# A hybrid layer's RWKV pairs: values centred while they are turned, a gate in rounded products, and eight steps joined to others

## What is computed

```python
g = jax.nn.sigmoid(gd) @ f32(g2)                 # gate, rank 160
...
y = wkv7_scan(rh, heads(decay), kh, vh, -kk, kk * ah)
mean = jnp.mean(y, axis=-1, keepdims=True)       # over the 64 of a head
var = jnp.mean(jnp.square(y - mean), axis=-1, keepdims=True)
y = (y - mean) * lax.rsqrt(var + LNX_EPS)
y = y.reshape(B, L, D_RWKV) * f32(lnx_w) + f32(lnx_b)
bonus = jnp.sum(rh * kh * f32(r_k), axis=-1, keepdims=True) * vh
y = (y + bonus.reshape(B, L, D_RWKV)) * g
```

## Time and profile before

| | |
|---|---|
| median of 3 runs | 2562.8 us (2559.62 to 2563.7) |
| the profiled execution | 2557.35 us |
| its span | 2555.8 us |
| PE busy | 2460.7 us, 96% |
| DVE, ACT, POOL busy | 1131.4, 792.2, 170.0 us |
| mean granted clock of PE | 0.986 of full |

### The profile page before, as it was taken

How to read it: one execution, slowest core, us unless ns; L and a number is a source line. 1 busy time by engine, 2 the same in 40 slices (tenths; PEclk the granted TensorE clock), 3 DMA queues, 4 the chain that set the end, 5 groups by cost and what they waited for, 6 DMA issues and landing times.

```text
span 2555.8 us, 44106 instructions
## 1 busy us (share of the span) xinstructions
PE 2460.7 (96%) x16486; PEld 2067.5 (81%) x16486; DVE 1131.4 (44%) x1721; ACT 792.2 (31%) x1306; POOL 170.0 (7%) x190
## 2 busy tenths in 40 slices
PE   6999999999999779999999999999999999999997
PEld 6988888889888658888888888888888888888886
DVE  6356466475574654453333333233333333332343
ACT  6434334244243322243222132232232222221333
POOL 3001011010010012200000000000000000000033
PEclk8999999999999889999999999999999999999999
DMA  7242342332423443333323323333233233233332
GB/s 202 72 91 72 85 93 75 86 85 70 92 73 92 103 143 105 92 89 108 91 82 107 90 87 103 90 96 101 82 102 95 82 107 91 86 103 90 95 95 91
DMA packets 502951, 242.08 MB, mean 95 GB/s; under 512 B 98400, under 2 KB 495840, under 8 KB 502304
## 3 DMA queue, kind: packets, MB, share of 16 engines
q1 hardware_dynamic: 498352, 226.10, 32.6%
q0 software_dynamic: 4480, 14.17, 1.6%
HBM read 223.29 MB, written 16.92 MB: 94 GB/s over the span
## 4 chain that ended last, share of the span: by engine, by line
PE 81%; DVE 10%; DMA 3%; ACT 2%; issue 2%; SPq 1%; DVEq 0%; ACTq 0%
PE PD L1293 63%; PE PD L1296 12%; DMA uni<-inverse 1%; DVE uni L1104 1%; DVE uni L976 1%; DMA inverse<-UU 1%; PE PW L1408 1%; DMA yin<-mixed 1%; DVE w_lo L902 1%; DVE uni L1049 0%; DVE uni L1043 0%; DVE act_lo L907 0%; PE PW L1415 0%; PE PW L1454 0%; PE PW L1353 0%
## 5 line engine op out<-in xcount | busy, mean ns | idle before, releaser
L902 DVE TENSOR_TENSOR w_lo<-w_raw,w_hi 128x512 fp32r<-128x512 f32 x780 | 556.1, 749 | 305.4 <-ACT w_hi L650 294.0
L650 ACT CAST w_hi<-w_raw 128x512 fp32r<-128x512 f32 x780 | 456.5, 619 | 752.4 <-PE PD L1293 484.6
L1293 PE MATMUL PD<-act_hi,w_hi 128*128 128x512 f32 x1408 | 557.6, 396 | 5.2 <-DVE act_lo L951 5.2
L1293 PE MATMUL PD<-act_lo,w_hi 128*128 128x512 f32 x1408 | 558.4, 397 | 0.0
L1293 PE MATMUL PD<-act_hi,w_lo 128*128 128x512 f32 x1408 | 555.4, 394 | 0.0
L1293 PE MATMUL PD<-u_hi,w_hi 128*128 128x512 f32 x1024 | 409.7, 400 | 0.0
L1293 PE MATMUL PD<-u_hi,w_lo 128*128 128x512 f32 x1024 | 403.3, 394 | 0.0
L1293 PE MATMUL PD<-u_lo,w_hi 128*128 128x512 f32 x1024 | 401.5, 392 | 0.0
L1296 PE MATMUL PD<-act_hi,w_hi 128*128 128x264 f32 x1376 | 312.7, 309 | 11.4 <-DVE act_lo L907 10.2
L1293 PEld LDWEIGHTS PD<-act_hi,w_hi 128*128 128x128 f32 x1408 | 265.8, 189 | 70.3 <-DVE act_lo L951 6.4
L1293 PEld LDWEIGHTS PD<-act_lo,w_hi 128*128 128x128 f32 x1408 | 265.5, 189 | 61.7 <-issue 0.7
(11 more groups left out here) (251 smaller groups left out, 1464.9 us busy)
## 6 DMA issues: line engine op xcount, KB each, us to landing
w_raw<-in_w_up SPq DMA_DIRECT2D x256, 256.0 KB, 3.1
w_raw<-in_w_down SPq DMA_DIRECT2D x256, 256.0 KB, 2.9
w_raw<-in_w_in SPq DMA_DIRECT2D x200, 256.0 KB, 3.0
w_raw<-in_w_out SPq DMA_DIRECT2D x64, 256.0 KB, 2.7
x_rows<-in_x SPq DMA_DIRECT2D x4, 1024.0 KB, 8.0
residual<-res POOLq DMA_DIRECT2D x2, 2048.0 KB, 11.3
out<-rows SPq DMA_DIRECT2D x8, 512.0 KB, 4.9
uni<-inverse SPq DMA_DIRECT2D x16, 240.0 KB, 4.2
```

The lines of the kernel that those rows point to most:

```text
L650: nc.scalar.copy(w_hi[:, q % RING], w_raw[:, q % RAW]).then_inc(hi_split, 1)
L902: V.tensor_tensor(w_lo[:, q % RING], w_raw[:, q % RAW], w_hi[:, q % RING].bitcast(F32), ALU.subtract).then_inc(lo_split, 1)
L1293: ins = M(pd_seq(n), w, v[:, k, first:first + SEQ], start=begin, stop=end)
```

## The change

- PE turns the values by a product with `centre` (identity less the head mean) where it transposed them. The step `mean`, ACT's copy of y and DVE's `yc` go; ACT squares y out of PSUM, and `y1` reads y from PSUM.
- The gate's two fp32 products become four fp32r products (high by high, high by low, low by high, and the last 32 rows with their three parts stacked as one). They move into the step `var`, behind the variance's product and ahead of its signal. ACT and DVE split the gate's weights for each pair (`ghi`, `glo`). The 32 tail columns are loaded three times (12 loads for 4 at the start, three for one in each pair).
- `bsum`, `btr` and `ktr` become `tr`; `atr` and `mv` become `amv`; `tt16` goes into `t16`, `e` into `gh`, `mean` goes and `gate` goes into `var`.
- `lnb` is added to the bonus by ACT (`bonb`), so DVE's `y3` goes. A root on one number (`for_sqrt`) is put ahead of `sq`.
- DVE shifts the values in `ss`, behind `ssm`. PE's `ss` now also waits for DVE's `kk`.
- `PACE` places steps anew: `ss` 2, `low` 6, `vtr` 11, `gram0` 24, `tr` 26, `gram1` 29, `amv` 31, `x16` 54, `gh` 67, `y0` 72, `z8` 88, `y` 91, `var` 96.

```diff
-PACE = dict(ss=2, low=4, vtr=5, ahead0=5, gram0=7, bsum=1, btr=1, atr=1, ktr=1, gram1=1, mv=2, base1=0, base2=1,
-            ahead1=1, ahead2=4, ahead3=4, ahead4=4, ahead5=5, x16=2, t16=2, tt16=1, x32=2, tt32=2, pq=3, gh=3, e=1, y0=5,
-            z2=3, z3=2, z4=1, z5=2, z6=1, z7=2, z8=2, y=2, mean=3, var=4, gate=4)
+PACE = dict(ss=2, low=4, vtr=5, ahead0=6, gram0=7, tr=2, gram1=3, amv=2, base1=0, base2=0, ahead1=2, ahead2=4,
+            ahead3=4, ahead4=4, ahead5=4, x16=5, t16=2, x32=3, tt32=2, pq=3, gh=3, y0=5, z2=4, z3=2, z4=2, z5=2, z6=2,
+            z7=2, z8=2, y=3, var=5)
...
-ACT_STEPS = ["sq", "nrm", "for_sig", "sigw", "siga", "for_exp", "vtok", "epv", "em", "ep", "gs", "btok", "atok", "ktok", "mv", "x16", "x32",
-             "warm", "pq", "y", "sqc", "std"]
+ACT_STEPS = ["for_sqrt", "sq", "nrm", "for_sig", "sigw", "siga", "for_exp", "vtok", "epv", "em", "ep", "gs", "ghi", "btok",
+             "ktok", "bonb", "atok", "mv", "x16", "x32", "warm", "pq", "sqc", "std"]
 DVE_STEPS = (["kk", "ssm", "inv", "ld", "scan", "mid", "mu", "epv", "gs", "kkn", "tfac", "kp",
-              "at", "b", "bt", "rt", "kt", "rb", "gram0", "bon", "gram1", "diag"]
+              "at", "b", "bt", "rt", "kt", "rb", "gram0", "bon", "glo", "gram1", "diag"]
              + [f"{s}{m}" for m in (2, 4, 8) for s in ("pr", "ar", "pl", "al")] + ["ut"]
-             + ["t16", "tt16", "tt32", "gt", "hb", "e", *Z_STEPS, "yc", "inv2", "y1", "y2", "y3", "y4"])
+             + ["t16", "tt16", "tt32", "gt", "hb", "e", *Z_STEPS, "inv2", "y1", "y2", "y4"])
...
-SPLIT_FIRST = ("low", "base1", "base2", "x16", "y", "mean", "var")
-
-
-
-OUT_PACE = dict(pq=1, gh=1, z2=1, z3=1, z4=1, z5=1, z6=1, z7=1, z8=1, mean=2, var=2, gate=2)
+SPLIT_FIRST = ("low", "base1", "base2", "x16", "y", "var")
+
+
+
+OUT_PACE = dict(pq=1, gh=1, z2=1, z3=1, z4=1, z5=1, z6=1, z7=1, z8=1, y=2, var=4)
...
     low_wa = m_sb("low_wa", [P, T])
-    low_g = m_sb("low_g", [P, T])
-    low_g2 = m_sb("low_g2", [GATE_TAIL, T])
+    low_r = lambda name, n: sb(name, [P, n], F32R, on=mix)
+    low_hi, low_lo, low_tail = low_r("low_hi", SEQ), low_r("low_lo", SEQ), low_r("low_tail", SEQ)
     wa_w = m_sb("wa_w", [P, P])
     g_w = m_sb("g_w", [P, P])
-    g_w2 = m_sb("g_w2", [GATE_TAIL, P])
+    g_w2 = m_sb("g_w2", [P, P])
+    g_hi, g_lo, g_tail = low_r("g_hi", P), low_r("g_lo", P), low_r("g_tail", P)
...
-    ybuf, ycen = uni[:, 4 * W:4 * W + SEQ], uni[:, 4 * W + SEQ:4 * W + 2 * SEQ]
+    ycen = uni[:, 4 * W + SEQ:4 * W + 2 * SEQ]
+    low_g, low_g2 = em, epv[0:TAIL]
...
         sp.wait_ge(raw_zeroed, 1)
         for first, width in ((LOWR + 2 * P, GATE_TAIL), (LOWR, P), (LOWR + P, P)):
             for a in range(4):
-                load(win_q[a, :, :, first:first + width], q, width=width)
+                for copy in range(0, TAIL if width == GATE_TAIL else 1, GATE_TAIL):
+                    load(win_q[a, :, :, first:first + width], q, first=copy, width=width)
...
+        const(nc.gpsimd.tensor_tensor(centre[:], ident[:], head_mean[:], ALU.subtract))
...
-            pool.dma_start(g_w2[:], gate_g2[P:P + GATE_TAIL, bass.ts(j, P)]).then_inc(g_loaded, 16)
+            for first in range(0, TAIL, GATE_TAIL):
+                pool.dma_start(g_w2[first:first + GATE_TAIL, :], gate_g2[P:P + GATE_TAIL, bass.ts(j, P)]).then_inc(g_loaded, 16)
...
-            act.wait_ge(raw_loaded[q % RAW], at(16 * (q // RAW + 1), 16 * per // RAW, it))
+            act.wait_ge(raw_loaded[q % RAW], at(16 * (q // RAW + 3), 16 * per // RAW, it))
...
                 if name == "ss":
+                    done("for_sqrt", nc.scalar.activation(warm[:], eps_t[:, 0:1], ACT.Sqrt))
                     done("sq", nc.scalar.activation(fsq, zk[:], ACT.Square, scale=feat("k_k")))
...
-                if name == "btr":
-                    pe("btr")
-                    done("btok", nc.scalar.copy(b_tok[:].rearrange("p c n -> p (c n)"), turned(0)))
-                if name == "atr":
-                    pe("atr")
+                if name == "ahead0":
+                    act.wait_ge(g_loaded, at(64, 64, j))
+                    nc.scalar.copy(g_hi[:], g_w[:])
+                    done("ghi", nc.scalar.copy(g_tail[:], g_w2[:]))
+                if name == "tr":
+                    pe("tr")
+                    done("btok", nc.scalar.copy(b_tok[:].rearrange("p c n -> p (c n)"), in_row(0)))
+                    done("ktok", nc.scalar.copy(k_tok[:].rearrange("p c n -> p (c n)"), in_row(1)))
+                    dve("bon")
+                    done("bonb", nc.scalar.activation(bonus[:], bonus[:], ACT.Identity, bias=feat("lnb")))
+                if name == "amv":
+                    pe("amv")
                     done("atok", nc.scalar.copy(AMV[:, :, :, 0:HS], PW[:, 2:4, 0:W].rearrange("p h (c n) -> p h c n", c=SLOTS)))
-                if name == "ktr":
-                    pe("ktr")
-                    done("ktok", nc.scalar.copy(k_tok[:].rearrange("p c n -> p (c n)"), turned(0)))
-                if name == "mv":
-                    pe("mv")
                     done("mv", nc.scalar.copy(AMV[:, :, :, HS:P], PW[:, 0:2, 0:W].rearrange("p h (c n) -> p h c n", c=SLOTS)))
...
-                    done("y", nc.scalar.copy(token_order(ybuf), by_bank(2)))
-                if name == "mean":
-                    dve("yc")
-                    done("sqc", nc.scalar.activation(ysq, ycen, ACT.Square))
+                    done("sqc", nc.scalar.activation(token_order(ysq), by_bank(2), ACT.Square))
                 if name == "var":
                     pe("var")
-                    done("std", nc.scalar.activation(ysq, PW[:, 2, :], ACT.Sqrt, bias=eps_t[:, 1:2]))
+                    done("std", nc.scalar.activation(ysq, PW[:, 0, :], ACT.Sqrt, bias=eps_t[:, 1:2]))
...
+            if n == 3:
+                dve.wait_ge(low_top, 1)
+                r = slice(2 * GATE_TAIL, TAIL)
+                V.tensor_tensor(low_tail[r, :], low_g2[r, META:T], low_tail[r, :].bitcast(F32), ALU.subtract).then_inc(low_done, 1)
+            if n == 4:
+                dve.wait_ge(low_top, 2)
+                V.tensor_tensor(low_lo[:], low_g[:, META:T], low_hi[:].bitcast(F32), ALU.subtract).then_inc(low_done, 1)
...
+                    dve.wait_ge(z_done, at(5, 3, j))
                     done("kk", V.tensor_scalar(kk, zk[:], feat("k_k"), None, ALU.mult))
                     pe("ss")
                     done("ssm", V.tensor_scalar(halves(fsq), pw(2), 1e-24, None, ALU.max))
+                    shift(5, zv[:, PAD:TP], par[:, bass.ds(j + (PAR["mu"] + 16), 1)], 3, j)
                     act("nrm")
                     done("inv", V.reciprocal(fsq, fsq))
...
+                if name == "tr":
+                    pe("tr")
+                    done("bon", V.tensor_tensor(bonus[:], PW[:, 3, :], zv[:, PAD + META:TP], ALU.mult))
+                    act("ghi")
+                    r = slice(GATE_TAIL, 2 * GATE_TAIL)
+                    V.tensor_tensor(g_tail[r, :], g_w2[r, :], g_tail[r, :].bitcast(F32), ALU.subtract)
+                    done("glo", V.tensor_tensor(g_lo[:], g_w[:], g_hi[:].bitcast(F32), ALU.subtract))
...
-                if name == "mean":
-                    pe("mean")
-                    done("yc", V.tensor_tensor(ycen, ybuf, PW[:, 0, :], ALU.subtract))
                 if name == "var":
                     act("std")
                     done("inv2", V.reciprocal(ysq, ysq))
-                    done("y1", V.tensor_tensor(ycen, ycen, ysq, ALU.mult))
-                    done("y2", V.tensor_scalar(ycen, ycen, feat("lnw"), feat("lnb"), ALU.mult, ALU.add))
-                    done("y3", V.tensor_tensor(ycen, ycen, bonus[:], ALU.add))
-                if name == "gate":
-                    pe("gate")
-                    done("y4", V.tensor_tensor(bt[:, PAD + META:TP], ycen, PW[:, 0, :], ALU.mult))
+                    done("y1", V.tensor_tensor(token_order(ycen), by_bank(2), token_order(ysq), ALU.mult))
+                    act("bonb")
+                    done("y2", V.scalar_tensor_tensor(ycen, ycen, feat("lnw"), bonus[:], ALU.mult, ALU.add))
+                    done("y4", V.tensor_tensor(bt[:, PAD + META:TP], ycen, PW[:, 1, :], ALU.mult))
...
+                    dve("kk")
...
-                    ins = turn(0, lambda cols: zv[:, cols])
+                    pe.wait_ge(z_done, at(6, 3, j))
+                    for k in range(SLOTS):
+                        ins = M(PW[:, k // 4, k % 4 * P:(k % 4 + 1) * P], zv[:, k * P:(k + 1) * P], centre[:], start=True, stop=True)
...
+                if name == "tr":
                     dve("gram0")
-                    ins = M(PW[:, 2, :], same_head[:], ld[:, 0:SEQ], start=True, stop=True)
-                if name == "btr":
-                    ins = turn(0, lambda cols: bt[:, cols])
-                if name == "atr":
-                    dve("bon")
+                    M(PW[:, 3, :], same_head[:], ld[:, 0:SEQ], start=True, stop=True)
+                    for i in range(2 * SLOTS):
```

(58 more changed lines are left out.)

42 lines of the change are left out of this document (18 added, 24 removed).

## The result

The changed kernel took 2575.8 us (median of 5, 2574.12 to 2576.37) against 2562.8 us (median of 5, 2559.62 to 2566.66) for the kernel before: ratio 1.0051, 95% interval 1.0036 to 1.0066. It is 13 us slower. I had forecast 2561 with a range up to 2571; the case "slower" had 0.24. The span of the profiled run of after is 2574.8 us, that of before 2555.8 us. That is 19 us, more than the medians show, because the profiled run of before was 5.4 us under its median and that of after lies at its median.

The account below looks back on a forecast made before the run. PE's work (96% busy) and `var`'s place against the next pair bound it. Six loop intervals +3.3, first pair -5, last pair +5, -4, -2, start +0.5: -2 on 2557.35, 2555; median 5.4 above, 2561; range 2546 to 2571.

Parts of the forecast that it names:

- the case "slower": Rival: late chain delays `gram0`, the gram exchange and `x16`; decides from 1.0 us per pair, +9, 2570; chance 0.24.
- The wait at ss: T is when PE has made its 96 k-steps; PE waits 6.0 us for `kk`, `ss` starting at T + 9.3.
- From ss to gram0: PE's work and DVE's chain each take 19.5 us between `ss` and `gram0`; lower clock adds 1.9 in each pair.
- clock does not cost it: Rival: lower stretches fall inside the wait or `gram0` has reserve; seven pairs save 1.9 each, -13, 2548; chance 0.20.
- They meet: At `gram0`, PE's work and DVE's chain both arrive 19.5 us behind `ss`, so PE's wait there goes.
- From gram0 to the next T: Clean pair: `ss` to the next T (PE's 96 k-steps made) takes 91.1 us, of which 19.5 lie ahead of `gram0`.
- Less 1.4 (of 1.5 at `x16`, to which PE now has 23 k-steps): At `x16`: 1.4 of the 1.5 us wait goes, with 23 k-steps from `amv` where it had 21 from `mv`.
- the joined steps: Five joins of PE steps save 0.9 us a pair together, with 0 and 1.6 as ends.
- a sign of being wrong: Wrong if waits at `ss` were under 4 us, the clock stayed up, or `x16` still waited 1.5 us.
- The first pair: No `var` ahead, so no wait for `kk`: -6.1 us, taken as -5 since its `gram0` wait may have been smaller.
- The last pair: `x16` near T + 58: +5; `y` ahead of the last two loads: -4; work behind `y`: -2.
- joined steps save more: Rival: joins reach the upper bound of 1.6, with cheaper entries of `x16` and `y0`: -8, 2553; chance 0.18.

Follow-up runs that it names:

- e1: The changed kernel with `var` (variance's product and gate) three k-steps ahead of the pair's end; 2555.9 us, ratio 0.9982 to the kernel before.
- e9: The changed kernel with `var` three k-steps earlier, `ss` waiting for `y1` instead of `kk`, and the gate behind the k-steps following `var`; 2528.5 us, ratio 0.9864.
- e8: The changed kernel with `x16` and everything from it to `gh` one k-step later, taken out ahead of `y0`; 2574.6 us, ratio 1.0041.
- e11: The changed kernel with one join undone: `tt16`'s 32 small products in a step of their own one k-step behind `t16`; 2581.2 us, ratio 1.0068.
- e5: The kernel before the change with one wait more: its `ss` waits for `kk`; 2572.8 us, ratio 1.0044.
- e6: The changed kernel with `ss` waiting for `y1`, last reader of y's banks, by its own count instead of for `kk`; 2551.8 us, ratio 0.9959.
- e7: The changed kernel with the gate's four products in a step of their own behind `var`, so `std` waits for the variance's product alone; 2566.2 us, ratio 1.0017.

## Why the prediction was wrong, by its own steps

By the medians the kernel takes 15 us more than forecast (2575.8 against 2561). By the two profiled executions it is 21: the sum came to -2, and the span grew by 19, with some 5 us of that because the profiled execution of before was a quick one. The steps below go by the traces.

**The wait at ss: right.** Predicted: `ss` at T + 9.3, a wait of 6.0 us in seven pairs. Measured: T + 9.67, and 42.0 us in seven pairs with the 5.2 behind the jump.

**From ss to gram0: right, clock included.** 19.5 and 1.9 for the clock made 21.4; measured 21.76. Both parts are borne out: without a lower stretch it is 19.8 (e1's pair from 728.59, e9's 19.90), with it 1.9 more. The rival "clock does not cost it" is out. The Trainium skill (TensorE: Matmul & The Clock Gate, Part 1) has a kernel in which every wait for data is followed by a throttled stretch with a cost of its own. The trace agrees: behind each of the seven waits the clock fell, for 1.9 us, and in e9 this is gone with the wait. "They meet" at `gram0` was right as well: its waits are 0.2 at the most.

**From gram0 to the next T: the step that failed.** Predicted 71.6 (91.1 less 19.5), measured 73.36 (the pair 104.79 less 9.67 and 21.76). "Less 1.4 (of 1.5 at `x16`, to which PE now has 23 k-steps)" counted a gain twice. Beside it I took off 0.8 behind `gram0` and the joined steps (three of the five lie ahead of `x16`, some 0.5). Those bring PE to `x16` earlier, and `x16` stands where the inverse lands: 29.5 us behind `gram0` in the clean pair of before (366.94 below, less the 337.41 of the earlier trace rows), 29.60 in after with two k-steps more ahead of it, 29.63 in e8 with three more. The two k-steps filled 1.5 us of a wait of 1.5 to which 1.3 was added. So PE still waits there, 0.9 to 1.9 us (1.3 in the mean of seven) where 0.1 was forecast, close to the 1.5 that the prediction named as a sign of being wrong. PE's timeline of before in that pair:

```profile
366.94 0.69 PE L1389 MATMUL PW<-uni 64*64 64x64 f32 x32 [1.36 <-DMA uni<-inverse]
```

`t16`'s 0.3 to 0.4 for ACT's copy is a new wait, and takes back what the join of `tt16` gives (e11: 0.33).

A smaller term was put at nothing without a reason. The forecast compared a pair that is clean but for the stretch behind `ss` with the mean of before, 101.75, which lies 0.6 over its clean pairs because two have a lower stretch. After has one again: from T = 312.70 `gram0` to T is 74.84, with a lower clock behind the wait of 1.89 at `x16`; in the other five it is 72.9 to 73.4. So of the 1.76 about 0.3 is that stretch, and 1.5 the double count with `t16`'s wait.

Per pair of the loop: 0.36 + 0.36 + 1.76 = 2.5 us over the forecast of 102.3, 15 us in six.

**The first pair**: predicted -5, measured -2.9 (T at 208.76 against 211.33, less the 0.3 of the start below), the same double count once.

**The last pair**: predicted -1, measured about +4. T to the end of `y4` was 108.9 us (821.82 to 930.69) and is 112.6 (837.50 to 950.13). PE's timeline has `x16` there:

```profile
897.08 1.12 PE L1409 MATMUL PW<-uni 64*64 64x64 f32 x32 [4.03 <-DMA uni<-inverse]
```

And the chain of work, up to `y4`:

```profile
920.44 3.81 DMA yin<-mixed
924.27 0.63 ACT act_hi L722
...
929.91 2.65 DMA yin<-mixed
...
935.11 2.56 PE PD L1318 x6
937.67 1.29 PE PW L1480 x32
...
949.44 0.70 DVE bt L1135
```

`x16` came 59.6 behind T, +6.6 where I had +5. `y` followed 40.6 later against 41.1, -0.5 where I had -4. That two splits of y move behind it is right: of the fifteen splits of loaded slices thirteen stand ahead of the last ZB that `y` needs, where it was all fifteen, and the fifteenth began 4.1 us behind the thirteenth (914.78 and 910.67). Two things that had no term take it back. The thirteenth split came 37.6 behind `x16` and not 35.9, and one of the loads took 3.81 us. And `OUT_PACE` now puts two k-steps of the first output tile ahead of `y`, 2.56 us at the lower clock, where before `y` followed that ZB at once: from the last split ahead of `y` to `y` it is 3.0 us against 1.1. Behind `y` it was 14.8 us and is 12.5, -2.3 where I had -2.

**The start**: `ss` of the first pair at 114.16 against 113.86, +0.3; I had 0.5.

**The rivals.** "Slower: the late chain reaches further than gram0" named a piece of what happened: `ss` at the lower clock takes 2.13 us instead of 1.16, and the second reciprocal starts at T + 13.5 where my chain gave T + 11.9 (9.3 + 1.1 + 1.5), more than the 1 us that the rival asked for. But that shifted `gram0` by only 0.7 (T + 31.4 against T + 30.7), under the 1.0 from which the rival decides. The greater part of the miss lies behind `gram0` and in the last pair. Joined steps were worth 0.33 for the one that was measured, which is the size of "joined steps save more"; taken as five that is 1.6 a pair, but where a join lies ahead of a fixed time it is lost again.

**What remains open**: why e5's pairs have more lower stretches behind `x16`, why the load from 920.44 took 3.81 us, and what the 1.6 us behind the jump in e9 are.

The cause of the slowdown itself is shown. What the change saves is real, but smaller than it looks: `gram0` to T is 4.4 us shorter a pair than before (73.36 against 77.77), with 0.73 of that a k-step that now stands ahead of `gram0` and 0.86 the variance's product, now behind T. It is outweighed by 5.9 us more between T and `ss` and 1.6 more between `ss` and `gram0` (the k-step, the centring and the clock, less the wait at `gram0` that is gone). Most of the gap came from two orders that the change didn't need: a wait for a later step than the one that frees the banks (e6, 24 us), and the signal of `var` behind the gate (e7, 9 us). With these two mended and `var` three k-steps earlier (e9), the same change is 1.4% faster than the kernel before.

## What to carry to other kernels

A saving on an engine counts only up to the next moment that the engine does not set: before adding savings, mark such moments (here the inverse's landing, some 29.5 us behind `gram0`), and sum separately between them. When a buffer's copy is dropped and its readers keep the bank, make the next writer wait for the last reader by a count of its own, not for the last step of a list. And in a loop in which a chain on other engines follows one signal, work ahead of the signal is added to the pair and work behind it covers the chain: the same four products cost nothing or 9 us by their place alone.
